# A two-layer transformer trunk on one core: every buffer start moved to a multiple of 512 bytes

## The reference: what is computed

```
for i in range(2):
    h = rms_norm(x, attn_norm[i])
    x = x + (fox_mixer if i == 0 else swa_mixer)(h, ...)      # w_in, attention, w_out
    h = rms_norm(x, ffn_norm[i])
    gate, up = split(h @ w_up[i])                             # 2048 x 11264
    x = x + (silu(causal_conv3(gate)) * up) @ w_down[i]       # 5632 x 2048
```

## The kernel before, in words

| buffers | start modulo 512, before | after the change |
|---|---|---|
| `xk`, `hs`, all `raw`, `whi`, `wlo`, `ident`, `gains` | 128 | 0 |
| `conv` | 384 | 256 |
| `rln`, `rbc` | 288 | 160 |
| `sqj`, `hf`, `gbuf` | 416 | 288 |
| `ybuf` | 448 | 320 |
| the region: `gs`, `oT` and the attention's larger buffers | 448 | 0 |

## Time and profile before

### The profile page before, as it was taken

The page is one execution under the profiler, slowest core; times in us unless marked ns, Lnnn a source line. Parts: engine busy times, 40 slices in busy tenths (PEclk is TensorE's granted clock), DMA queues, the critical chain, the costliest instruction groups (busy, mean ns, idle before and its releaser), DMA issues.

```text
span 2242.8 us, 31777 instructions
## 1 busy us (share of the span) xinstructions
PE 2201.7 (98%) x11808; PEld 1875.7 (84%) x11808; DVE 1313.6 (59%) x1557; ACT 1041.0 (46%) x1365; POOL 3.9 (0%) x9
## 2 busy tenths in 40 slices
PE   6999999999999999999999998999999999999999
PEld 5888888888888888888887887778888888888887
DVE  4545545557667666754444676456766676664443
ACT  5445544544444444444444565444444444443332
POOL 0000000000000000000000000000000000000000
PEclk9999999999999999999999999999999999999999
DMA  6555554556565656555555432455565666655554
GB/s 194 151 142 151 151 148 144 178 160 197 178 196 179 196 177 197 182 194 185 188 183 180 151 123 94 134 178 178 181 195 185 191 182 195 184 191 188 188 188 159
DMA packets 239152, 388.95 MB, mean 173 GB/s; under 512 B 12860, under 2 KB 85340, under 8 KB 239068
## 3 DMA queue, kind: packets, MB, share of 16 engines
q1 hardware_dynamic: 238432, 387.52, 55.9%
q10 hardware_dynamic: 636, 0.28, 0.0%
HBM read 385.65 MB, written 2.10 MB: 173 GB/s over the span
## 4 chain that ended last, share of the span: by engine, by line
PE 97%; DVE 1%; ACT 1%; issue 0%; DMA 0%; ACTq 0%; DVEq 0%
PE ps L1029 37%; PE ps L1039 30%; PE ps L1035 19%; PE ps L1143 1%; PE ps L1145 1%; PE ps L1146 1%; PE ps L1206 1%; PE ps L1296 1%; PE ps L1117 1%; PE ps L1258 1%; PE ps L1292 1%; ACT whi L562 0%; PE ps L1267 0%; PE ps L1297 0%; DVE wlo L783 0%
## 5 line engine op out<-in xcount | busy, mean ns | idle before, releaser
L1029 PE MATMUL ps<-hs,whi 128*128 128x512 f32 x3632 | 929.0, 398 | 0.5 <-DVE wlo L783 0.5
L783 DVE TENSOR_TENSOR wlo<-raw,whi 128x1024 fp32r<-128x1024 f32 x376 | 460.0, 1224 | 529.8 <-ACT whi L562 529.8
L1029 PEld LDWEIGHTS ps<-hs,whi 128*128 128x128 f32 x3632 | 659.1, 190 | 126.3 <-issue 5.3
L562 ACT ACTIVATE whi<-raw 128x1024 fp32r<-128x1024 f32 x378 | 400.0, 1060 | 499.0 <-PE ps L1039 378.9
L789 DVE TENSOR_TENSOR wlo<-raw,whi 128x1024 fp32r<-128x1024 f32 x352 | 425.3, 1222 | 289.8 <-ACT whi L569 289.7
L569 ACT ACTIVATE whi<-raw 128x1024 fp32r<-128x1024 f32 x352 | 371.5, 1061 | 470.8 <-PE ps L1035 470.8
L1035 PEld LDWEIGHTS ps<-hs,wlo 128*128 128x128 f32 x3616 | 494.4, 191 | 35.9
L1035 PE MATMUL ps<-hs,wlo 128*128 128x256 f32 x3616 | 504.7, 282 | 0.0
L1039 PE MATMUL ps<-whi,gs 128*128 128x512 f32 x1408 | 357.9, 396 | 0.0
L1039 PEld LDWEIGHTS ps<-whi,gs 128*128 128x128 f32 x1408 | 264.4, 188 | 63.3
L1039 PE MATMUL ps<-wlo,gs 128*128 128x512 f32 x704 | 193.2, 395 | 0.0
(11 more groups left out here) (143 smaller groups left out, 1076.8 us busy)
## 6 DMA issues: line engine op xcount, KB each, us to landing
raw<-in_ffn_w_up SPq DMA_DIRECT2D x352, 512.0 KB, 4.2
raw<-in_ffn_w_down SPq DMA_DIRECT2D x176, 512.0 KB, 3.6
raw<-in_fox_w_in SPq DMA_DIRECT2D x98, 512.0 KB, 3.7
raw<-in_swa_w_in SPq DMA_DIRECT2D x40, 512.0 KB, 3.6
raw<-in_fox_w_out SPq DMA_DIRECT2D x32, 512.0 KB, 3.6
raw<-in_swa_w_out SPq DMA_DIRECT2D x32, 512.0 KB, 3.6
xk<-in_x SPq DMA_DIRECT2D x8, 256.0 KB, 7.0
out_x<-xk SPq DMA_DIRECT2D x8, 256.0 KB, 4.5
```

The source lines that it names most:

```text
L562: act.activation(whi[slot][:, :], raw[slot][:, :], ACT.Copy).then_inc(hi_ready, 1)
L783: tt(wlo[slot][:, :], raw[slot][:, :], whi[slot][:, :].bitcast(F32), ALU.subtract).then_inc(lo_ready, 1)
L1029: return pe.matmul(ps[:, bank, :], whi[slot][:, c:c + P], moving.rearrange("p h t -> p (h t)"), start=first, stop=last)
```

## The change

The counter starts at a multiple of 512 instead of 64, and it is rounded up to a multiple of 512 again before the region.

```
-        place = [nc.sbuf_base + (-nc.sbuf_base) % 64]
+        place = [nc.sbuf_base + (-nc.sbuf_base) % 512]
...
         ybuf = sb("ybuf", [P, 4, T])
+        place[0] += -place[0] % 512
         region = place[0]
```

## The result

The kernel with the change takes 2227.66 us (median of 4 runs, 2227.23 to 2228.19), the kernel before in the same measurement 2244.77. The ratio is 0.9922 with a 95% interval of 0.991 to 0.9935: 17 us faster. The prediction said no difference, 2244.2 us, and its range ended at 2234 on the fast side.

The account below looks back on a forecast made before the run. TensorE's matmul streaming was taken as the bound, busy 2201.7 of 2242.8 us. Four terms of 0 left the span at 2242.8 us; the forecast against the median was 2244.2 us, range 2234 to 2250.

Parts of the forecast that it names:

- What bounds the kernel: Whole kernel: TensorE's matmuls, busy 2201.7 of 2242.8 us; 0.23 to 0.24 us of each unit is not one column per cycle.
- the term for streamed operands: TensorE's matmuls streaming `hs`, `whi`, `wlo`: moving them to residue 0 changes nothing, 0 us, between -88.6 and +39.6.
- all faster cases together: Whole kernel: the cases faster by more than 0.2%, chance 0.07 + 0.04 + 0.02 = 0.13.
- The bound of -88.6 us: All 11808 matmuls: the most gained if 7.5 ns each, independent of columns, were the price of a badly placed start.
- Loads of the held operand: TensorE's loads in lines 1029, 1039, 1145: 188 to 192 ns at residues 128 and 448, so term 0.
- VectorE, ScalarE and DMA: VectorE/ScalarE work and DMA into `raw` and `xk`: two terms of 0, each with ends -2 and +2 us.
- Equal residues are better: Line 1039's 2880 matmuls: unequal held and streamed residues cost 3.35 ns each; 9.6 us faster, 2234.6; chance 0.04.
- A start off the boundary costs each matmul something: All matmuls: a streamed start at residue 128 costs one piece more; up to 88.6 us faster, 2155.6; chance 0.07.
- Everything on one residue collides: Line 1039: reads of held and streamed operands, both at residue 0, now meet; +9.6 us, 2253.8; chance 0.06.

Follow-up runs that it names:

- e16: Against the change: `wlo` alone moved to residue 64, `hs`, `whi` and `gs`/`oT` at 0, so one stage has two distances; 2229.42 us.
- e8: As the change, all at residue 0, except the four `raw` buffers at 320; 2227.62 us (one run).
- e1: First half of the change alone: counter starts at a multiple of 512, region follows without a gap, held `gs`/`oT` still 320 past streamed `whi`/`wlo`; 2245.19 us.
- e7: Against the change: `gs`/`oT` and `hs` at residue 256, `whi`/`wlo` at 0, so held is 256 past streamed in both patterns; 2227.51 us (one run).
- e3: Against the kernel before: only the region moved, to residue 128, equal to that of `whi`/`wlo`; 2227.74 us, ratio 0.9928.
- e4: Against the change: everything at residue 64 instead of 0, so residues are equal and no buffer is at a multiple of 128; 2227.60 us.
- e2: Second half of the change alone: `whi`/`wlo` stay at residue 128, only the region moves, to 0; 2241.02 us, ratio 0.9987.
- e5: Against the change: held operand 64 bytes past streamed in both patterns (`whi`/`wlo` at 0, `gs`/`oT` at 64, `hs` at 448); 2233.89 us (one run).
- e15: Against the change: held operand 160 bytes past streamed in lines 1029 and 1035, 96 past in line 1039; 2261.54 us (one run).
- e9: Against the change: held operand 192 bytes past streamed in both patterns (`whi`/`wlo` at 0, `gs`/`oT` at 192, `hs` at 320); 2212.34 us (one run).
- e13: Against the change: `whi`/`wlo` 192 past `hs` in lines 1029 and 1035, `gs`/`oT` still at distance 0 in line 1039; 2209.48 us, ratio 0.9845.

## Why the prediction was wrong

*What bounds the kernel:* right. TensorE's pace is the time, and 8 to 9% of each unit was something other than one column per cycle. The prediction said that an effect of addresses would have to be in there, and it was.

*The step that failed* is the term for streamed operands, taken at 0. Its own bounds, -88.6 and +39.6 us, held the truth, and the choice within them did not. The term measures 2880 x 0.00665 = 19.2 us, of which the stages of line 1039 show 18.3. The forecast put at 0 an unknown that its own bounds left open by 128 us, and gave all faster cases together 0.13.

The choice rested on one comparison: units with equal residues take 2.79 us and units with unequal ones 2.80, both for 6144 columns. It compared two things that differ in more than the residue, and two effects hid each other. With equal distance of 0 a unit of the down projection takes 12 x 226.7 ns = 2.72 us, 0.08 less than before. The up projection at the same distance takes 2.79, because it alternates 8 matmuls of 512 columns with 8 of 256. By the starts in the trace its 512-column steps are 233, 236, 228, 232, 231 and then three times 227 ns, before and after the change alike: after the shorter matmuls it takes five matmuls to come to 227, the step that the changed down projection has throughout. In e16 a change of distance brings nearly the same row of steps (231, 236, 228, 232, 231, 227). The prediction named the different mix as a reason for 3.35 ns and did not see that the same mix could hide another 3.3.

The bound of -88.6 us rested on 7.5 ns per matmul that do not depend on the columns, from a line through the means 118.75 and 230.0 ns, and both means hold disturbed steps. The steps to which the up projection settles at distance 0 are 120 ns for 256 columns and 226.7 for 512, each 13.3 ns more than one column per cycle at 2.4 GHz.

*Loads of the held operand:* the rows were right and asked of the wrong instrument. Those loads take 188 ns at distance 0 and at 320 alike; the price is in the step from matmul to matmul, which this view does not show. A mean that stays the same does not clear a resource that two instructions share.

*VectorE, ScalarE and DMA:* their terms of 0 held, and e8 shows that the position of `raw` has no part in it.

*The rivals.* "Equal residues are better" had the right place and the right sign, with 0.04 as its chance and 9.6 us as its price. What it stated for line 1039, that different starts of the two operands cost time, is what e1 to e7 show; that the distance counts modulo 256, and that some unequal residues beat equal ones in the up projection, it did not have. The price was half: it took 3.35 ns from the difference to line 1029, whose 230 ns are themselves not undisturbed. "A start off the boundary costs each matmul something" is refuted by e3 and e4. "Everything on one residue collides" had the same two operands and the wrong sign.

What is shown: the pace of TensorE depends on the distance modulo 256 between the operand being held and the one being streamed, with different values for places 32 bytes apart, and on the matmuls just before. What is argued only: that the two reads get in each other's way. The trace has a load of a held operand start 2 to 5 ns after the start of nearly every 512-column matmul of the up and down projections, so both run together. The Trainium skill says, in "TensorE: Matmul & The Clock Gate", section "Step-by-step: what each phase is for", that the two reads have ports of their own and the load takes nothing from the running matmul. These kernels show up to 7.6 ns per matmul that depends on where one lies against the other (226.7 at 0, 234.3 at 96), so for these float32 operands the measurement decides against that sentence, if a meeting of the reads is the cause.

A rival is left. ScalarE and VectorE write `whi` and `wlo`, and no run moves their writes apart from TensorE's reads. The traces speak against it: in the last down projection the steps that lie wholly in time in which neither engine works (103 to 148 of the 1055) average 231.6 ns in the kernel before, 232.3 in e2, 234.9 in e5 and 234.4 in e15, against 226.4 with the change. The slow pace is there without them. No kernel tests this by itself, nor a form of the matmuls without the load beside them.

## What to carry to other kernels

Where TensorE is the bound, the starts of its held and its streamed buffers are a parameter to be swept, against each other and not against a power of two. With starts at multiples of 32 bytes and a period of 256 there are eight distances; finer ones were not tried, and all of this is one kernel, in which every matmul of 256 or 512 columns has a load of its own. The best is not the same for every pattern (0 for long runs of 512 columns, 192 or 64 where lengths of 512 and 256 alternate), and pads of a few hundred bytes gave 1.5% here, twice what the rule "all at multiples of 512" gave. When two paths through a trace come out equal, ask whether they are equal in all but the thing in question, before equality is read as no effect.

## What the runs showed of the hardware

- Some mean steps recur. At the granted clock of 1.00, the level of 2.4 GHz, 226.7 ns are 544 cycles and 233.3 ns are 560, for 512 columns: 32 and 48 cycles over. The 113.3 and 120 ns steps for 256 columns in the starts of line 1035 are 272 and 288: 16 and 32 over. It is no grid: the means 228.9, 232.4 and 234.3 lie elsewhere, and single steps of down projections run from 224 to 241 ns.
- The pace has a memory. In e9 and e13 the units of an up projection, with the same instructions and the same distances, take 2.74 and 2.77 us in turn. In the kernel before, steps of 231 and 236 ns (235 or 230 by rounding) take turns through a down projection. In e5 the first of the two units of values for each pair of heads (first attention) has a mean step of 115.2 and 119.6 ns in turn from the second pair on, with the same instructions at the same distance.
- Moving the start of `raw` from 128 past a multiple of 512 to a multiple of 512 did not change how fast DMA writes it beyond 1%: 18.8 and 19.0 GB/s for each busy engine, for packets of 2048 bytes, whose median duration is 84 ns in both kernels.
